# A two-block transformer layer on one core: projections as one 512-column matmul per high weight tile instead of two of 256, with VectorE adding the two PSUM halves

## The chip, the core and the metric

The kernel runs on one core of one Trainium2 chip. The metric is the time of one execution in device microseconds (us). The core's engines work side by side: TensorE (PE in the profile; PEld is its loading of weights), VectorE (DVE), ScalarE (ACT), GpSimd (POOL), and SyncE (SP), which only issues transfers. Weights come from HBM by DMA into SBUF; TensorE writes its sums to PSUM, 8 banks of 512 float32 columns on 128 partitions.

## The reference

A sequence of 256 positions with 2048 features goes through two transformer blocks. Each normalizes x, projects it to many heads, runs several attention or recurrence branches, mixes them with gates, and adds the result to x. The first block also has a feed-forward part with a convolution over three positions. Cut to what matters here:

```python
h = rmsnorm(x, norm_attn[l])
... = jnp.split(h @ w_in[l], split_at, axis=-1)     # 2048 x (some 120 column blocks of 128)
o_nsa, o_sb, o_hg = nsa_mixer(...), stick_breaking(...), hgrn2(...)
merged = jnp.sum(gsig * jnp.einsum('btnc,ncd->btnd', branches, w_branch[l]), axis=2)
x = x + merged @ w_out[l]
u = rmsnorm(x, norm_ffn[l]) @ w_up[l]                # 2048 x 11264
c = conv_b + sum(shifted(u, j) * conv_w[j] for j in range(3))
x = x + (silu(gate) * val) @ w_down[l]               # gate, val = split(c)
# second block: rms_norm, h @ w_in_2, four attention kinds, gates, w_branch_2, w_out_2, final norm
```

All is float32 and must come out nearly so.

## The kernel before

**Products in three parts.** TensorE takes its operands as float32r (a reduced float32). To keep the precision, each weight tile w and each activation tile h is split into a high and a low part, w = whi + wlo and h = HH + HL. A product is whi·HH + whi·HL + wlo·HH. `mm3` (L511 to L515) issues these three matmuls for one weight tile of 128 x 128: L513 (whi with the high activations), L514 (whi with the low ones), L515 (wlo with the high ones), each with 256 columns, since an activation tile is 128 features x 256 positions. Each loads its 128 x 128 weights first (LDWEIGHTS in the profile), so whi is loaded twice.

**Blocks.** All weights are laid out in 470 blocks of 128 x 2048 floats (1 MB), streamed through a ring of 4 slots. Block n holds 16 weight tiles. In a projection of 2048 features (KT = 16 tiles) one block gives 128 output columns: 16 calls of `mm3`, 48 matmuls, summed in one half of a PSUM bank, `gps[0]` or `gps[1]` in turn (named gemm in the profile). That is the inner loop of `project` (L522 on). `pair` and `early` do the same for the first blocks after a normalization, on the activations before their factor (UH, UL in place of HH, HL); `early` puts some of its blocks in the banks M (mix). Other products (w_branch with 8 feature tiles, w_down, w_branch_2 with 4) also use `mm3`.

**What goes with a block.** SyncE issues the load of block n+4 when TensorE is done with block n (`reload`, semaphore gemm_done). ScalarE makes whi of block n+3 from the loaded block (L943, `split`), then takes the finished sum of block n out of PSUM (`take`: L966, L981, L992 with a sigmoid, or L1262 for w_up), which counts the semaphore evac_done. VectorE makes wlo of block n+3 (L1413). TensorE starts block n once wlo of it is there (lo_ready) and the sum of block n-2, which was in the same bank, is out (evac_done). The order on each engine is fixed by the program: `advance(k)` on each engine's side does k blocks' worth of this upkeep between pieces of attention work, and each engine takes its instructions strictly in order.

**Where the projection's result goes elsewhere.** For w_out the sum is added to x by VectorE (`residual`, L1711). For w_up (88 blocks) ScalarE takes the centre tap of the convolution out of PSUM (L1262) and VectorE the two others (L1765, L1766). The first 8 blocks of w_in, w_up and w_in_2 go through VectorE's `early`: a multiplication by the norm's factor on the way out of PSUM (L1465).

**Other places named below.** The linear recurrence (hgrn2) runs in 8 levels with HG_STEP = 3 blocks beside each; L1669, L1670 end it, and `operand` (L1678) makes the low parts of the branches' outputs. The norm's sums of squares are L1477, L1478, its factor L1441, the low part of the normalized activations L1448.

## Time and profile before

| | |
|---|---|
| median of 3 runs | 2945.47 us (2942.90 to 2945.55) |
| span of the profiled execution, first to last instruction | 2942.8 us |
| TensorE matmuls | busy 2867.0 us, 97% of the span, 23642 recorded |
| weight loads | busy 2842.7 us |
| VectorE | busy 1622.2 us, 55% |
| ScalarE | busy 1306.6 us, 44% |
| DMA | 545.92 MB, mean 186 GB/s |

The profiled execution's own time is its span and 2 to 3 us around it: the runs' median lies 2.7 us above the span. A matmul's duration in the profile is a latency: the next one starts long before it ends. How fast TensorE works is read from start to start. "Idle before" names what an engine waited for.

### The profile page before, as it was taken

The numbers are of one execution on the slowest core, as the hardware profiler recorded it, in microseconds if no ns is written. First come the engines' busy times: TensorE is split into PE (matmuls) and PEld (weight loads), VectorE is DVE, ScalarE is ACT, GpSimd is POOL, SyncE is SP. The second block draws the span as 40 slices with busy tenths as digits, with TensorE's granted clock in tenths as the row PEclk, the third lists the DMA queues.
The fourth block names the chain that finished last, engine by engine and source line by source line (L and its number), as shares of the span: only waits on it lengthen the run. The fifth ranks groups of instructions, "written<-read, shape, count | busy, mean of one in ns | idle before, by whom it ended". The sixth has DMA issues, their size and how long they took to land.

```text
span 2942.8 us, 55782 instructions
## 1 busy us (share of the span) xinstructions
PE 2867.0 (97%) x23642; PEld 2842.7 (97%) x23642; DVE 1622.2 (55%) x1573; ACT 1306.6 (44%) x1387; POOL 159.7 (5%) x125
## 2 busy tenths in 40 slices
PE   7897999999999999999999999999999999999997
PEld 6897899999999999999999999999999999999997
DVE  6443544466544677766666545554444554546575
ACT  3353446664443444444444333343334444445442
POOL 4000000000000001000000000010000000000330
PEclk9999899999999999999999999999999999999999
DMA  6556444445545655455554555455554455555853
GB/s 204 182 185 181 148 149 144 158 170 175 170 174 214 236 193 200 176 182 185 185 178 180 216 185 195 177 190 184 185 180 164 163 204 203 184 193 207 285 209 129
DMA packets 94836, 545.92 MB, mean 186 GB/s; under 512 B 11528, under 2 KB 25992, under 8 KB 34288
## 3 DMA queue, kind: packets, MB, share of 16 engines
q1 hardware_dynamic: 84768, 511.01, 49.0%
q0 software_dynamic: 9936, 32.92, 3.9%
q8 instruction: 111, 1.82, 0.2%
q14 instruction: 21, 0.17, 0.0%
HBM read 519.44 MB, written 24.38 MB: 185 GB/s over the span
## 4 chain that ended last, share of the span: by engine, by line
PE 93%; DVE 3%; DMA 3%; ACT 0%; issue 0%; DVEq 0%; SPq 0%; ACTq 0%
PE gemm L513 26%; PE gemm L515 26%; PE gemm L514 26%; PE mix L513 4%; PE mix L515 4%; PE mix L514 4%; DMA raw<-wstream 2%; DVE wlo L1413 1%; PE mix L760 1%; PE mix L600 1%; DMA XT<-xT 0%; PE mix L696 0%; PE mix L885 0%; ACT whi L943 0%; DVE cbuf L1765 0%
## 5 line engine op out<-in xcount | busy, mean ns | idle before, releaser
L1413 DVE TENSOR_TENSOR wlo<-raw,whi 128x2048 fp32r<-128x2048 f32 x470 | 1095.7, 2332 | 1069.2 <-ACT whi L943 1068.4
L513 PE MATMUL gemm<-HH,whi 128*128 128x256 f32 x5728 | 1634.1, 285 | 15.6 <-issue 10.8
L514 PE MATMUL gemm<-HL,whi 128*128 128x256 f32 x5728 | 1623.4, 283 | 0.0
L515 PE MATMUL gemm<-HH,wlo 128*128 128x256 f32 x5728 | 1623.4, 283 | 0.0
L943 ACT ACTIVATE whi<-raw 128x2048 fp32r<-128x2048 f32 x470 | 898.6, 1912 | 1388.5 <-DMA raw<-wstream 1385.3
L513 PEld LDWEIGHTS gemm<-HH,whi 128*128 128x128 f32 x5728 | 1101.9, 192 | 22.1 <-issue 14.8
L514 PEld LDWEIGHTS gemm<-HL,whi 128*128 128x128 f32 x5728 | 1102.3, 192 | 0.7 <-issue 0.7
L515 PEld LDWEIGHTS gemm<-HH,wlo 128*128 128x128 f32 x5728 | 1101.8, 192 | 0.0
L513 PE MATMUL mix<-ACTH,whi 128*128 (+1 forms) x528 | 149.4, 283 | 0.0
L514 PE MATMUL mix<-ACTL,whi 128*128 (+1 forms) x528 | 149.4, 283 | 0.0
L515 PE MATMUL mix<-ACTH,wlo 128*128 (+1 forms) x528 | 149.4, 283 | 0.0
L513 PE MATMUL gemm<-OH,whi 128*128 128x256 f32 x384 | 108.7, 283 | 0.0
L514 PE MATMUL gemm<-OL,whi 128*128 128x256 f32 x384 | 108.7, 283 | 0.0
L515 PE MATMUL gemm<-OH,wlo 128*128 128x256 f32 x384 | 108.7, 283 | 0.0
L513 PEld LDWEIGHTS mix<-ACTH,whi 128*128 128x128 f32 x528 | 101.4, 192 | 0.0
L514 PEld LDWEIGHTS mix<-ACTL,whi 128*128 128x128 f32 x528 | 101.4, 192 | 0.0
L515 PEld LDWEIGHTS mix<-ACTH,wlo 128*128 128x128 f32 x528 | 101.4, 192 | 0.0
L513 PE MATMUL gemm<-UH,whi 128*128 128x256 f32 x192 | 57.6, 300 | 22.3 <-DVE wlo L1413 16.9
L513 PEld LDWEIGHTS gemm<-OH,whi 128*128 128x128 f32 x384 | 73.7, 192 | 0.0
L514 PEld LDWEIGHTS gemm<-OL,whi 128*128 128x128 f32 x384 | 73.7, 192 | 0.0
L515 PEld LDWEIGHTS gemm<-OH,wlo 128*128 128x128 f32 x384 | 73.7, 192 | 0.0
L513 PE MATMUL mix<-YH,whi 128*128 128x256 f32 x256 | 72.4, 283 | 0.0
(363 smaller groups left out, 2666.1 us busy)
## 6 DMA issues: line engine op xcount, KB each, us to landing
raw<-wstream SPq DMA_DIRECT2D x470, 1024.0 KB, 4.9
scratch<-gate_scratch POOLq DMA_DIRECT2D x12, 512.0 KB, 5.2
gate_scratch<-scratch SPq DMA_DIRECT2D x32, 128.0 KB, 3.9
GL<-gate_scratch POOLq DMA_DIRECT2D x8, 512.0 KB, 5.1
gate_scratch<-arena SPq DMA_DIRECT2D x32, 128.0 KB, 3.8
bias_scratch<-arena POOLq DMA_DIRECT2D x1, 3328.0 KB, 45.9
btile<-bias_scratch POOLq DMA_DIRECT2D x21, 128.0 KB, 2.4
XT<-xT SPq DMA_DIRECT2D x4, 512.0 KB, 9.0
```

The source lines that it names most:

```text
L513: pe.matmul(ps, whi[slot][:, w], mh, start=first, stop=False, **kw)
L514: pe.matmul(ps, whi[slot][:, w], ml, start=False, stop=False, **kw)
L515: return pe.matmul(ps, wlo[slot][:, w], mh, start=False, stop=last, **kw)
L600: return pe.transpose(ps, src, ident[p0:p0 + n, p0:p0 + n])
L760: ins = pe.matmul(M[:, i // 4, (i % 4) * P:(i % 4) * P + P], x, x, start=True, stop=True)
L943: f(whi[slot][:, :], raw[slot][:, :], ACT.Copy).then_inc(s["hi_ready"], 1)
L1413: tt(wlo[slot][:, :], raw[slot][:, :], whi[slot][:, :].bitcast(F32), ALU.subtract).then_inc(s["lo_ready"], 1)
```

## The change

For every projection of 16 feature tiles, the two matmuls on whi become one: the high and the low activation tile are streamed one behind the other, 512 columns, against one load of whi. Their products land in the two halves of a PSUM bank. wlo with the high activations (256 columns) is added to the first half, as before. `mm2` does this; to allow a single access pattern over both tiles, HH and HL (and each UH, UL) become parts of one tensor, HX (UX). The products of w_branch, w_down and w_branch_2 keep `mm3`.

The two halves then have to be added. VectorE does it in `join`, a tensor_reduce over pairs that lie 256 columns apart, as it takes the sum out of PSUM. So all the evictions that ScalarE did for these projections move to VectorE, and stand in its order ahead of wlo of block n+3. In the sigmoid case ScalarE still applies the sigmoid, in SBUF. For w_up VectorE joins into `btile`, and ScalarE and VectorE read the taps from there. `early` joins first and multiplies then, and `residual` adds in two steps. GpSimd's load of one bias row into `btile` waits until w_up is done. HG_STEP goes from 3 to 4.

```diff
-HG_STEP = 3
+HG_STEP = 4
-        HH = at("HH", [P, KT, T], o_hh, F32R)
-        HL = at("HL", [P, KT, T], o_hl, F32R)
+        HX = at("HX", [P, 2 * KT, T], o_hh, F32R)
+        HH, HL = HX[:, 0:KT, :], HX[:, KT:2 * KT, :]
...
+        def halves(bank):
+
+            return bank.rearrange("p (c t) -> p t c", c=2)
...
+            pool.wait_ge(s["f_taps"], N_UP)
             bias(R_FOX, i)
...
+            def mm2(bank, w, mh, mx, slot, first, last):
+
+                def high():
+                    return pe.matmul(bank.rearrange("p (c t) -> p c t", c=2), whi[slot][:, w], mx, start=first, stop=last)
+
+                def low():
+                    return pe.matmul(bank[:, 0:T], wlo[slot][:, w], mh, start=False, stop=False)
+
+                if last:
+                    low()
+                    return high()
+                high()
+                return low()
...
+                            if kt == KT:
+                                ins = mm2(gps[bank][:, :], cols(k), mh(k), ml(k), slot, k == 0, k == KT - 1)
+                            else:
+                                ins = mm3(gps[bank][:, c * T:(c + 1) * T], cols(c * kt + k),
+                                          mh(k), ml(k), slot, k == 0, k == kt - 1)
...
+            def xk(k):
+                return HX[:, k::KT, :]
...
             def to_scratch(began):
+
                 def take(n, bank, i, j, it):
-                    act.wait_ge(s["gemm_done"], n + 1)
-                    f(tile(i + dst0), gps[bank][:, 0:T], ACT.Copy).then_inc(s["evac_done"], 1)
+
+                    c = i + began
+                    act.wait_ge(s["evac_done"], c + (use(B_G0) + 1))
+                    d = SCR[:, c * T:(c + 1) * T] if isinstance(i, int) else SCR[:, bass.ds(c * T, T)]
+                    f(d, d, ACT.Sigmoid).then_inc(s["g0_sig"], 1)
                 return take
...
+            stages = ((0, B_G0, lambda i: None), (B_G0, B_Y, to_scratch), (B_B, B_Y2, lambda i: None))
...
+            def join(dst, bank):
+
+                return dve.tensor_reduce(dst, halves(bank), AX, ALU.add)
+
+            def to_arena(dst0):
+                def take(n, u0, i, j):
+                    dve.wait_ge(s["gemm_done"], n + 1)
+                    join(tile(i + dst0), gps[(u0 + j) % 2][:, :]).then_inc(s["evac_done"], 1)
+                return take
...
-                    tt(A[:, j, :] if take is None else btile[j % 2][:, 0:T], early_bank(r, j), rstd[:, :], ALU.mult
-                       ).then_inc(s["evac_done"], 1)
+                    d = A[:, j, :] if take is None else btile[j % 2][:, 0:T]
+                    me.link(join(d, early_bank(r, j)))
+                    tt(d, d, rstd[:, :], ALU.mult).then_inc(s["evac_done"], 1)
...
-                    tt(d, d, gps[(u0 + j) % 2][:, 0:T], ALU.add).then_inc(s["evac_done"], 1)
+                    bank = gps[(u0 + j) % 2]
+                    me.link(tt(d, d, bank[:, T:2 * T], ALU.add))
+                    tt(d, d, bank[:, 0:T], ALU.add).then_inc(s["evac_done"], 1)
...
+                    dve.wait_ge(s["gemm_done"], it * 4 + (B_UP + j + 1))
+                    join(btile[j % 2][:, 0:T], gps[(u0 + j) % 2][:, :]).then_inc(s["evac_done"], 1)
                     ahead(it * 4 + (B_UP + j), (B_UP + j) % RING, it + (B_UP + j) // RING)
+                    dve.wait_ge(s["evac_done"], it * 4 + (u + j + 1))
```

On TensorE, the first weight tiles of the program (UH and UL are the high and low activations, whi and wlo the weight parts) stand so before:

```order
L513 MATMUL gemm<-UH_80,whi_53 128x256
L514 MATMUL gemm<-UL_83,whi_53 128x256
L515 MATMUL gemm<-UH_80,wlo_57 128x256
L513 MATMUL gemm<-UH_80,whi_53 128x256
L514 MATMUL gemm<-UL_83,whi_53 128x256
L515 MATMUL gemm<-UH_80,wlo_57 128x256
```

and now, at the end of the first block and the start of the next (UX holds both activation parts):

```order
L527 MATMUL gemm<-UX_79,whi_53 128x512
L530 MATMUL gemm<-UX_79,wlo_57 128x256 x2
L527 MATMUL gemm<-UX_79,whi_53 128x512
L527 MATMUL gemm<-UX_79,whi_54 128x512
L530 MATMUL gemm<-UX_79,wlo_58 128x256
```

Three instructions per weight tile become two with the same 768 columns in sum; in a block's last tile the low part goes first.

On VectorE, after the first norm factor of the feed-forward part (its `early`, where btile receives a block's product and cbuf the convolution) before:

```order
L1441 RECIPROCAL rstd<-rstd 128x256
L1465 TENSOR_TENSOR btile_89<-gemm,rstd 128x256
L1765 SCALAR_TENSOR_TENSOR cbuf<-btile_89,vec,cbuf 128x255
L1766 SCALAR_TENSOR_TENSOR cbuf<-btile_89,vec,cbuf 128x254
L1465 TENSOR_TENSOR btile_90<-gemm,rstd 128x256
L1413 TENSOR_TENSOR wlo_58<-raw_50,whi_54 128x2048
```

and now:

```order
L1486 RECIPROCAL rstd<-rstd 128x256
L1432 TENSOR_REDUCE btile_85<-gemm 128x256
L1512 TENSOR_TENSOR btile_85<-btile_85,rstd 128x256
L1811 SCALAR_TENSOR_TENSOR cbuf<-btile_85,vec,cbuf 128x255
L1812 SCALAR_TENSOR_TENSOR cbuf<-btile_85,vec,cbuf 128x254
L1432 TENSOR_REDUCE btile_86<-gemm 128x256
L1512 TENSOR_TENSOR btile_86<-btile_86,rstd 128x256
L1407 TENSOR_TENSOR wlo_58<-raw_50,whi_54 128x2048
```

One tensor_reduce (the join) stands ahead of each multiplication, and wlo behind it.

In the loop over the other 80 blocks of w_up, VectorE's block before (register instructions between):

```order
L1413 TENSOR_TENSOR wlo_57<-raw_49,whi_53 128x2048
L1764 REGISTER_ALU
L1765 ISA
L1765 SCALAR_TENSOR_TENSOR cbuf<-gemm,vec,cbuf 128x255
L261 ISA
L1766 ISA
L1766 SCALAR_TENSOR_TENSOR cbuf<-gemm,vec,cbuf 128x254
```

and now:

```order
L1432 TENSOR_REDUCE btile_85<-gemm 128x256
L1406 REGISTER_ALU
L1407 TENSOR_TENSOR wlo_57<-raw_49,whi_53 128x2048
L1839 REGISTER_ALU
L1810 REGISTER_ALU
L1811 ISA
L1811 SCALAR_TENSOR_TENSOR cbuf<-btile_85,vec,cbuf 128x255
L267 ISA
L1812 ISA
L1812 SCALAR_TENSOR_TENSOR cbuf<-btile_85,vec,cbuf 128x254
```

The join comes first in the block, and the taps read btile in SBUF, no more the PSUM bank.

## Rows read from the trace of the kernel before

**Rows 1.** The page: busy time by engine, and the chain that ended last.
```profile
PE 2867.0 (97%) x23642; PEld 2842.7 (97%) x23642; DVE 1622.2 (55%) x1573; ACT 1306.6 (44%) x1387; POOL 159.7 (5%) x125
...
PE 93%; DVE 3%; DMA 3%; ACT 0%; issue 0%; DVEq 0%; SPq 0%; ACTq 0%
```
**Rows 2.** Page, costliest groups: out<-in, shapes, xcount | busy us, mean ns | idle before.
```profile
L1413 DVE TENSOR_TENSOR wlo<-raw,whi 128x2048 fp32r<-128x2048 f32 x470 | 1095.7, 2332 | 1069.2 <-ACT whi L943 1068.4
L513 PE MATMUL gemm<-HH,whi 128*128 128x256 f32 x5728 | 1634.1, 285 | 15.6 <-issue 10.8
L943 ACT ACTIVATE whi<-raw 128x2048 fp32r<-128x2048 f32 x470 | 898.6, 1912 | 1388.5 <-DMA raw<-wstream 1385.3
```
**Rows 3.** Matmul groups, shapes apart (weights 128*rows, output 128xcolumns); same columns.
```profile
L513 PE MATMUL gemm<-UH,whi 128*128 128x256 f32 x192 | 57.6, 300 | 22.3 <-DVE wlo L1413 16.9 <-DVE UL L1453 4.0 <-DVE XR L1815 1.4
L513 PE MATMUL mix<-UH,whi 128*128 128x256 f32 x192 | 54.6, 285 | 0.4 <-DVE wlo L1413 0.4
L515 PE MATMUL gemm<-HH,wlo 128*128 128x256 f32 x5728 | 1623.4, 283 | 0.0
```
**Rows 4.** Timeline of TensorE in a projection: start us, duration us.
```profile
700.00 0.28 PE L513 MATMUL gemm<-HH,whi 128*128 128x256 f32 x1
700.12 0.28 PE L514 MATMUL gemm<-HL,whi 128*128 128x256 f32 x1
700.24 0.28 PE L515 MATMUL gemm<-HH,wlo 128*128 128x256 f32 x1
```
**Rows 5.** Timeline of TensorE, float32r with 128 columns on 30 weight columns.
```profile
213.29 0.22 PE L629 MATMUL mix<-whi,blkH 128*30 128x128 f32 x1
213.35 0.22 PE L630 MATMUL mix<-whi,blkL 128*30 128x128 f32 x1
213.41 0.22 PE L631 MATMUL mix<-wlo,blkH 128*30 128x128 f32 x1
```
**Rows 6.** Timeline of TensorE, plain float32 with 512 columns.
```profile
173.41 5.31 PE L616 MATMUL mix<-scratch,cst 128*128 128x512 f32 x12
```
**Rows 7.** Matmul groups, the last float32r matmul before a wait (no load behind it).
```profile
L515 PE MATMUL gemm<-UH,wlo 128*128 128x256 f32 x1 | 0.3, 279 | 0.0
```
**Rows 8.** Busy us (xcount) of PE, PEld, DVE, ACT, POOL in windows; clock, DMA.
```profile
1300.00:1400.00 100.00, 100.00 (x836) 100.00 (x835) 64.60 (x79) 47.42 (x54) 0.00 (x0) 1.00 0.51 180
```
**Rows 9.** VectorE groups, shapes apart.
```profile
L1495 DVE TENSOR_REDUCE st<-scratch 128x2 f32<-128x512 f32 x12 | 8.2, 686 | 0.4
L1693 DVE TENSOR_TENSOR arena<-gemm,scratch 128x512 f32 x8 | 5.5, 692 | 18.5 <-PE gemm L515 18.5
L1711 DVE TENSOR_TENSOR arena<-arena,gemm 128x256 f32 x24 | 10.1, 420 | 32.9 <-PE gemm L515 32.9
```
**Rows 10.** VectorE's timeline in the loop over w_up, [idle before <-releaser].
```profile
1220.59 2.29 DVE L1413 TENSOR_TENSOR wlo<-raw,whi 128x2048 fp32r<-128x2048 f32 x1 [1.95 <-ACT whi L943]
```
**Rows 11.** VectorE's timeline, first blocks of w_up.
```profile
1156.13 4.17 DVE L1413 TENSOR_TENSOR wlo<-raw,whi 128x2048 fp32r<-128x2048 f32 x1
...
1164.40 2.28 DVE L1413 TENSOR_TENSOR wlo<-raw,whi 128x2048 fp32r<-128x2048 f32 x1
...
1187.04 1.22 DVE L1448 TENSOR_TENSOR HL<-arena,HH 128x1024 fp32r<-128x1024 f32 x1
```
**Rows 12.** TensorE's timeline, starts of blocks 5, 6 and 9 of w_up.
```profile
1160.35 0.39 PE L513 MATMUL mix<-UH,whi 128*128 128x256 f32 x1
...
1166.74 0.39 PE L513 MATMUL mix<-UH,whi 128*128 128x256 f32 x1 [0.38 <-DVE wlo L1413]
...
1184.12 0.35 PE L513 MATMUL gemm<-HH,whi 128*128 128x256 f32 x1
```
**Rows 13.** VectorE's timeline at the end of the recurrence.
```profile
817.34 2.35 DVE L1669 SCALAR_TENSOR_TENSOR arena<-arena,vec 128x2048 f32<-128x2048 f32 x1 [3.37 <-ACT arena L1197]
...
828.80 2.29 DVE L1678 TENSOR_TENSOR OL<-arena,OH 128x2048 fp32r<-128x2048 f32 x1 [1.98 <-ACT OH L1207]
```
**Rows 14.** VectorE's timeline, last block of the program.
```profile
2926.99 0.42 DVE L1711 TENSOR_TENSOR arena<-arena,gemm 128x256 f32<-128x256 f32 x1 [4.15 <-PE gemm L515]
```

More of the change, by code:

```diff
@@ L929, in _ @@
                 ins.then_inc(s["gemm_done"], 1)
-            pair(B_O2, s["mg_l"], [(N_Y + i + 1, 4 * i + 4) for i in range(N_Y2)], hk, lk)
-            project(B_O2 + 2, N_O - 2, hk, lk)
+            pair(B_O2, s["mg_l"], [(N_Y + i + 1, 4 * i + 4) for i in range(N_Y2)], hk, xk)
+            project(B_O2 + 2, N_O - 2, hk, xk)
             norm_sums(3)
@@ L1177, in _ @@
             decays(0)
-            advance(3)
+            advance(HG_STEP)
             for lv in range(1, 8):
@@ L1249, in conv @@
             def conv(n, bank, i, j):
-                first = isinstance(i, int) and i < EARLY
-                if first:
-                    act.wait_ge(s["evac_done"], use(B_UP) + i + 1)
-                else:
-                    act.wait_ge(s["gemm_done"], n + 1)
-                product = btile[j % 2][:, 0:T] if first else gps[bank][:, 0:T]
+                act.wait_ge(s["evac_done"], i + (use(B_UP) + 1))
+                product = btile[j % 2][:, 0:T]
                 v0 = V_CONV + 4 * i
@@ L1419, in ahead @@
                 split(n + AHEAD, s2 % RING, turn + s2 // RING)
+            loop = [0]
             def plain(n0, count, u0=0, take=None, per=0):
@@ L1423, in body @@
                     if take:
+                        loop[0] = turn - (n0 + j) // RING
                         take(n, u0, i, j)
@@ L1431, in _, with to_gates @@
             at = [0]
[L1433 to L1436 removed]
+            def join(dst, bank):
[5 more added lines that the diff above has]
+                return take
+            def to_gates(n, u0, i, j):
+                dve.wait_ge(s["gemm_done"], n + 1)
+                join(gates[:, :], gps[(u0 + j) % 2][:, :]).then_inc(s["evac_done"], 1)
@@ new lines, in to_ring, with take @@
+            def to_ring(layer, began):
+                def take(n, u0, i, j):
+                    dve.wait_ge(s["gemm_done"], n + 1)
+                    r = (j + began) % 4
+                    turns = (j + began) // 4 + layer * 2 * N_G // 4
+                    if not isinstance(i, int):
+                        dve.wait_ge(gate_out[r], (loop[0] + turns) * 16)
+                    elif turns:
+                        dve.wait_ge(gate_out[r], turns * 16)
+                    join(gring[layer][r], gps[(u0 + j) % 2][:, :]).then_inc(s["evac_done"], 1)
+                return take
@@ new lines, in to_scratch, with take @@
+            def to_scratch(began):
+                def take(n, u0, i, j):
+                    dve.wait_ge(s["gemm_done"], n + 1)
+                    c = i + began
+                    if isinstance(i, int) and c >= 12:
+                        dve.wait_ge(gate_out[c % 4], 2 * N_G // 4 * 16)
+                    d = SCR[:, c * T:(c + 1) * T] if isinstance(i, int) else SCR[:, bass.ds(c * T, T)]
+                    join(d, gps[(u0 + j) % 2][:, :]).then_inc(s["evac_done"], 1)
+                return take
@@ new lines, in _ @@
+            stages = ((0, N_NSA - 1, to_arena), (N_NSA - 1, B_SB, lambda i: to_gates),
+                      (B_SB, B_CW, lambda i: to_arena(20 + i)), (B_CW, B_SB2, lambda i: None),
+                      (B_SB2, B_G, lambda i: to_arena(20 + N_SB1 + i)), (B_G, B_G0, lambda i: to_ring(0, i)),
+                      (B_G0, B_Y, to_scratch),
+                      (B_B, B_Z, to_arena), (B_Z, B_G2, lambda i: to_arena(58 + i)), (B_G2, B_Y2, lambda i: to_ring(1, i)))
+            def advance(count):
+                while count:
+                    first, end, take = [x for x in stages if x[0] <= at[0] < x[1]][0]
+                    n = min(count, end - at[0])
+                    plain(at[0], n, use(at[0]), take(at[0] - first))
+                    at[0] += n
+                    count -= n
@@ L1757, in taps @@
             def taps(u, i, j, pair):
-                first = isinstance(i, int) and i < EARLY
-                product = btile[j % 2][:, 0:T] if first else gps[(u0 + j) % 2][:, 0:T]
-                done = "f_taps" if first else "evac_done"
+                product = btile[j % 2][:, 0:T]
                 v0 = V_CONV + 4 * i
@@ L1772, in taps @@
                     me.link(tt(e[:, :], e[:, :], cbuf[:, b, 0, :], ALU.mult))
-                    dve.wait_ge(s[done], i + 1 if first else u + 1)
+                    dve.wait_ge(s["f_taps"], i + 1)
                     tt(cbuf[:, b, 0, :], e[:, :], cbuf[:, b, 1, :], ALU.mult).then_inc(s["f_act"], 1)
@@ L1996, in _ @@
             dve.wait_ge(s["x2_back"], 64)
-            plain(B_O2, N_O, use(B_O2), residual(3, XT2), 2)
+            plain(B_O2, N_O, use(B_O2), residual(3, XT2), 3)
             factor(3)
```

77 lines of the change are left out of this document (24 added, 53 removed).

## The prediction, made before the changed kernel was run

> **What bounds the kernel now.** I read the page's busy shares and the chain of waits first. TensorE is busy 97% of the span and holds 93% of the chain, VectorE 3% and DMA 3% [rows 1]. So what TensorE has to stream sets the time, and the other engines matter only where their work comes late. In the costliest groups the reader sees who is waited for: wlo (VectorE, 470 times 2.33 us) waits for whi nearly all of its idle time, and whi (ScalarE) waits for the loaded blocks [rows 2]. ScalarE and VectorE both have room.
>
> The second question is how long one matmul holds TensorE. Its duration of 0.28 us is a latency; in the timeline the next one starts 0.12 us later, whether it repeats the same whi with the low activations or takes wlo [rows 4]. The window of 100 us holds 836 of them [rows 8], 119.6 ns each, at granted clock 1.00 (the 2.4 GHz level). A weight tile's three matmuls are thus 360 ns and a block of 16 tiles 5.76 us. Per column that is 120/256 = 0.469 ns.
>
> **The change on TensorE.** The merged form stands where the projections have 16 feature tiles: 5728 + 192 + 192 = 6112 weight tiles [rows 2, 3], 382 blocks. Each gives up one weight load and one matmul instruction, and streams the same 768 columns. What a tile saves is therefore 240 ns less what one matmul of 512 columns takes from start to start. No row of before shows a float32r matmul of 512 columns, so I bound it.
>
> - Upper bound of the pitch, 240 ns (gain 0). The time goes with columns alone, if 0.469 ns is the rate at which float32r operands stream. The rows nearest to this: float32r matmuls of 128 columns, on only 30 weight columns, start 60 ns apart [rows 5], which is 0.469 ns per column again. Half the columns take exactly half the time; a fixed part per instruction, say 13 ns, would have made them 66. And a load of 30 columns instead of 128, for half the stream, has changed nothing in the rate, which it should if loads took read bandwidth from the stream.
> - Lower bound, about 213 ns, one column per 2.4 GHz cycle. For it: plain float32 matmuls of 512 columns, 12 instructions in 5.31 us [rows 6], at most 442 ns each, and if each passes the array twice, 0.43 ns per column and pass. So the array itself can go faster than 0.469. [...]
> - Between: the load slows the stream that it lies beside. The one float32r matmul with no load behind it lasts 279 ns against 283 [rows 3, 7]. If the 4 ns are the load's, the second half of the 512 columns, with no load beside it, saves some 4 to 14 ns: pitch 226 to 236.
>
> I take 240, since the row with half the columns is the same mode and excludes a fixed part. Term: 0. Each ns by which I am wrong is worth 6112 x 1 ns = 6.1 us; 4 to 14 ns are 24 to 86 us, 24 ns (216 instead of 240) are 147 us.
>
> The Trainium skill ("TensorE: Matmul & The Clock Gate", Back-to-back issue gap) states N/2.4 + 2.5 ns as the isolated spacing of a matmul with N columns. For 256 that is 109 ns, where the trace has 120 [rows 4]: it does not hold for this mode. By it the 512 columns would take 216. The same page (in its part on loading weights) says that weights have a read port of their own and take nothing from the running stream; the trace agrees as far as rows 5 reach, and it speaks against the case between.
>
> **The change on VectorE.** A join reads 512 columns from PSUM and writes 256. The trace has no such instruction. Nearest: a reduction of 512 columns from SBUF, 686 ns, and an addition over 512 columns out of PSUM, 692 ns [rows 9]. I take 0.69 us. The strided pairs could make it dearer, by at most about a factor of two (1.3 us, each half read on its own and the overhead paid twice); cheaper than the 0.42 us of a 256-column operation [rows 9] it can't be. The number, counted in the code: 213 evictions that ScalarE did for the projections, 80 of w_up and 24 in `early` make 317, x 0.69 = 219 us; the 32 residual blocks get a second addition, 32 x 0.42 = 13 us. VectorE goes from 1622 to about 1855 us, 63%. In the w_up loop, the fullest long stretch, it waits 1.95 us per block for whi [rows 10]; a join of 0.69, even of 1.3, fits in. It is hidden in steady stages: a block's bank is needed only one block (5.76 us) after the sum is done, and wlo(n+3) only three blocks after block n. ScalarE gets lighter, so whi comes no later.
>
> HG_STEP = 4 moves a block's upkeep earlier in each level of the recurrence, GpSimd's wait for f_taps moves a bias load behind w_up. Neither is on the path; the cover is TensorE's own stream of 23 us per 4 blocks. Term: 0.
>
> Not hidden, as wlo comes late already in these places:
> - The first blocks of w_up. After the late norm factor VectorE works off a backlog; one wlo takes 4.17 us there, and ends at 1160.30, where block 5 starts at 1160.35; block 6 starts at 1166.74, right behind the next wlo [rows 11, 12]. Two joins stand ahead of the first: 2 x 0.69 = +1.4; one more ahead of the second, +0.7. Both shift the program by about 2.1 us. Block 9 starts at 1184.12 and needs, for its last four tiles, the low activations that end at 1188.26; tile 12 is due at 1184.12 + 12 x 0.36 = 1188.44 [rows 11, 12], slack 0.2. Joins 2 to 8, seven, now stand ahead: 7 x 0.69 = 4.8, less the 2.1 shift and the slack: +2.5. Together some +5 us.
> - The end of the recurrence, where 2.35 and 2.29 us pieces and their ScalarE counterparts alternate [rows 13] and a join stands between: at most two joins, +1.3.
> - The last block of the program: the second addition lies bare, +0.4 [rows 14].
> - Other waits behind single joins (start of the attention parts, first block): +1, a guess from one or two joins of 0.69.
>
> Sum: 0 + 5 + 1.3 + 0.4 + 1 = about +8 us on the span of 2942.8, so 2951. The runs' median lies 2.7 above the profiled span, but the profiled execution itself is the fast end of them (2942.90), so in terms of the median I write 2952. With joins of 1.3 us the same sum gives about +13.
>
> **Rivals.**
> 1. The merged matmul streams at one column per cycle, 216 ns: -147, and +8 for the stalls: about 2806. For: the plain float32 rate [rows 6]. Against: rows 5, where half the columns take half of 120. By the skill's formula above this would be the result.
> 2. The load beside the stream costs something: pitch 226 to 236, -24 to -86 and +8: 2870 to 2930, centre 233 (-43), about 2910. For: 279 against 283 [rows 3, 7]; against: rows 5. These two end on the other side, faster. The point from which they decide is a pitch of 238.7 ns: below it the saving exceeds the 8 us.
> 3. Pitch 240, but the new stalls are absorbed (the backlog at w_up is caught by the block's own slack): 2943 to 2950, no change.
> 4. The join is much dearer than its neighbours in the trace. It becomes the bound of the w_up loop only above about 1.95 us, the idle time per block [rows 10]; for 80 blocks each 0.1 us beyond is 8 us. At 1.5 us it is not the bound but lengthens every backlog: w_up's first blocks +10, others +5: 2965 or more. Nothing in rows 9 speaks for it beyond the stride.
> 5. That the change doesn't do what it says: the order of instructions shows one instruction for two on every such tile, so only its price is open.
>
> **How the numbers follow.** Columns alone (pitch 240): 0.52, of which the stalls show as slower 0.33 (my forecast, 2952, own range 2946 to 2965), are absorbed 0.17, and 0.02 for a small gain from the freed ScalarE. Load beside stream: 0.27 (0.24 faster, 0.03 same). Full rate: 0.17. Dear join: 0.04. About 0.2% (6 us) is what a measurement of this kernel can tell from no change. Faster 0.02 + 0.24 + 0.17 = 0.43; same 0.17 + 0.03 = 0.20; slower 0.33 + 0.04 = 0.37. The range leaves out the full rate and the ends of the others: 2875 to 2972.
>
> **What would show it.** In a steady window of w_up the start-to-start of the 512-column matmul: 240 (forecast), 226 to 236, or 216. The pace of blocks there: 5.76, 5.54 to 5.7, or 5.38 us. The join's mean: 0.69. TensorE's idle time behind wlo at the start of w_up: some 5 us more. VectorE's wait for whi per block in w_up: about 1.3 instead of 1.95. A pitch below 238 ns, or joins over 1.3 us, makes the forecast wrong.

## The result: 2926.4 us, 17.8 us faster, from a gain of 41 us and a loss of 23

| | before | after |
|---|---|---|
| median | 2944.18 us | 2926.39 us (2920.17 to 2927.45) |
| ratio, 95% interval | | 0.9936 (0.9922 to 0.9950) |
| span of the profiled execution | 2942.8 us | 2925.6 us |

The page after: busy time by engine, and the groups that answer to [rows 1 to 3].

```profile
PE 2827.9 (97%) x17530; PEld 2518.4 (86%) x17530; DVE 1870.2 (64%) x1955; ACT 1250.5 (43%) x1159; POOL 154.5 (5%) x125
...
L527 PE MATMUL gemm<-HX,whi 128*128 128x512 f32 x5728 | 2027.6, 401 | 30.2 <-issue 12.3
L530 PE MATMUL gemm<-HX,wlo 128*128 128x256 f32 x5728 | 1555.1, 282 | 0.0
...
L1407 DVE TENSOR_TENSOR wlo<-raw,whi 128x2048 fp32r<-128x2048 f32 x470 | 1086.0, 2311 | 384.5 <-ACT whi L970 383.7
```

TensorE is as full as before, with 6112 matmuls and loads fewer. VectorE has 248 us more; the forecast was 233. Whether the stream got faster is again read from start to start. TensorE's timeline after, in the loop over w_up:

```profile
1300.00 0.40 PE L527 MATMUL gemm<-HX,whi 128*128 128x512 f32 x1
1300.24 0.28 PE L530 MATMUL gemm<-HX,wlo 128*128 128x256 f32 x1
1300.35 0.40 PE L527 MATMUL gemm<-HX,whi 128*128 128x512 f32 x1
...
1301.06 0.40 PE L527 MATMUL gemm<-HX,whi 128*128 128x512 f32 x1
```

Three tiles take 1.06 us, 353 ns each and not 360: over such a stretch the 512 columns hold TensorE 236 ns on average and the 256 of wlo 117. In the stretches with attention work between the blocks it is less, about 347 (231 + 116):

```profile
502.15 0.39 PE L527 MATMUL gemm<-HX,whi 128*128 128x512 f32 x1
502.38 0.28 PE L530 MATMUL gemm<-HX,wlo 128*128 128x256 f32 x1
502.50 0.39 PE L527 MATMUL gemm<-HX,whi 128*128 128x512 f32 x1
...
503.54 0.39 PE L527 MATMUL gemm<-HX,whi 128*128 128x512 f32 x1
```

The window that answers to [rows 8] holds 569 matmuls, two per tile, where 836 were three per tile; VectorE is at 77 us of 100, up from 65:

```profile
1300.00:1400.00 100.00, 100.00 (x569) 86.80 (x568) 77.22 (x99) 47.81 (x52) 0.00 (x0) 1.00 0.51 183
```

At 7 to 12 ns per tile, 6112 tiles give 43 to 73 us. Only 17.8 came out, so something took the rest. TensorE's waits after, by what ended them (us in total, times, longest):

```profile
PE gemm L527 <- DVE wlo L1407: 21.4, 3, 14.3
PE mix L723 <- ACT scratch L1119: 21.2, 1, 21.2
...
PE gemm L527 <- DVE arena L1432: 6.9, 2, 4.1
PE gemm L527 <- DVE scratch L1432: 6.0, 2, 3.4
...
PE mix L527 <- DVE wlo L1407: 3.2, 1, 3.2
PE mix L605 <- DVE gates L1538: 2.3, 1, 2.3
PE mix L627 <- DVE scratch L1987: 2.2, 1, 2.2
PE mix L656 <- DVE wlo L1407: 1.9, 1, 1.9
```

Before, the first two of these stood there with 19.5 and the same 21.2 us. The whole list adds up to 84.4 us, before to 62.4. The two rows on L1432, the join, are new: 12.9 us in four waits. The longest shows the mechanism. VectorE's timeline there, and TensorE's:

```profile
181.96 3.67 DVE L1572 SCALAR_TENSOR_TENSOR arena<-arena,vec,scratch 128x2048 f32<-128x2048 f32 x3 [8.60 <-ACT scratch L1070]
185.67 3.87 DVE L1584 TENSOR_TENSOR blkF<-arena,vec 128x240 f32<-128x240 f32 x8
189.44 0.69 DVE L1432 TENSOR_REDUCE arena<-gemm 128x256 f32<-128x512 f32 x1
```
```profile
190.28 0.77 PE L527 MATMUL gemm<-HX,whi 128*128 128x512 f32 x1 [4.10 <-DVE arena L1432]
...
191.06 0.63 PE L527 MATMUL gemm<-HX,whi 128*128 128x512 f32 x1
...
191.70 0.63 PE L527 MATMUL gemm<-HX,whi 128*128 128x512 f32 x1
```

VectorE takes its instructions in order. The join stands behind 7.5 us of attention work, the bank stays full, and TensorE waits 4.1 us for it. In the kernel before, the same pieces ran on VectorE (3.68 and over 3 us), but ScalarE emptied the bank in between, and TensorE did not wait:

```profile
185.58 1.90 ACT L943 ACTIVATE whi<-raw 128x2048 fp32r<-128x2048 f32 x1
187.38 0.37 ACT L966 ACTIVATE arena<-gemm 128x256 f32<-128x256 f32 x1
```

The wait has a second price, TensorE's clock. Behind the 4.1 us without work a pair takes 0.64 us from start to start (191.06 to 191.70), and not 0.35, until 193.6. The windows show the granted clock (the third figure from the end) there, and back at 1.00 behind it; the last line is the kernel before at the same time, without a wait:

```profile
190.00:192.00 2.00, 1.72 (x5) 1.56 (x6) 2.00 (x2) 1.41 (x2) 0.00 (x0) 0.55 0.29 123
...
194.00:196.00 2.00, 2.00 (x14) 1.75 (x13) 2.00 (x2) 0.00 (x0) 0.00 (x0) 1.00 0.04 8
```
```profile
190.00:192.00 2.00, 2.00 (x20) 2.00 (x18) 2.00 (x6) 2.00 (x3) 0.00 (x0) 1.00 0.19 33
```

So the granted clock fell from the 2.4 GHz level to the 1.2 GHz level. Five pairs took 3.34 us there in place of 1.77: this wait cost 4.1 us and then 1.6 us more. All four waits for a join in this execution have such a stretch beside them.

The time can be dated by blocks: SyncE issues the load of block n+4 the moment TensorE is done with block n. Difference to the kernel before, in us, at the end of some blocks (merge alone and joins alone are experiments below):

| end of block | time before | changed kernel | merge alone | joins alone | what lies between |
|---|---|---|---|---|---|
| 16 | 139.2 | -3.1 | -3.5 | -1.9 | |
| 26 | 201.9 | +1.5 | -4.3 | +3.6 | the wait shown above |
| 76 | 563.4 | -4.6 | -8.5 | +3.3 | attention |
| 84 | 617.0 | -0.7 | -9.8 | +6.6 | start of the recurrence |
| 124 | 883.2 | -2.7 | -15.6 | +10.2 | recurrence and its end |
| 166 | 1125.7 | -4.3 | -16.6 | +10.6 | w_branch, w_out |
| 178 | 1196.1 | -0.6 | -17.4 | +16.1 | first blocks of w_up |
| 256 | 1645.8 | -9.5 | -25.4 | +15.6 | rest of w_up |
| 300 | 1899.3 | -9.5 | -25.4 | +15.6 | w_down, unchanged |
| 396 | 2483.4 | -20.2 | -36.2 | +15.6 | second block's projections |
| 429 | 2692.4 | -16.9 | -41.7 | +20.4 | attention, its gates |
| 465 | 2904.1 | -17.2 | -42.2 | +23.1 | |

### The profile page after: what moved, and what is told of

It is laid out like the page before. It is cut to its first block, busy times and chain, and to the rows that moved or that the text cites. A ratio compares the mean times of both kernels' runs of the same rounds, so it can differ in the third digit from the quotient of the medians.

```text
span 2925.6 us, 43772 instructions
## 1 busy us (share of the span) xinstructions
PE 2827.9 (97%) x17530; PEld 2518.4 (86%) x17530; DVE 1870.2 (64%) x1955; ACT 1250.5 (43%) x1159; POOL 154.5 (5%) x125
## 4 chain that ended last, share of the span: by engine, by line
PE 91%; DVE 3%; DMA 3%; ACT 2%; issue 0%; POOL 0%; DVEq 0%; SPq 0%; ACTq 0%
PE gemm L527 46%; PE gemm L530 23%; PE mix L520 3%; PE mix L522 3%; PE mix L521 3%; DMA raw<-wstream 3%; PE gemm L521 2%; PE gemm L522 2%; PE gemm L520 2%; PE mix L527 1%; PE mix L787 1%; DVE wlo L1407 1%; PE mix L627 1%; PE mix L530 1%; ACT whi L970 0%
## 5 line engine op out<-in xcount | busy, mean ns | idle before, releaser
L527 PE MATMUL gemm<-HX,whi 128*128 128x512 f32 x5728 | 2027.6, 401 | 30.2 <-issue 12.3
L530 PE MATMUL gemm<-HX,wlo 128*128 128x256 f32 x5728 | 1555.1, 282 | 0.0
L527 PEld LDWEIGHTS gemm<-HX,whi 128*128 128x128 f32 x5728 | 1066.6, 189 | 266.8 <-issue 25.3
L530 PEld LDWEIGHTS gemm<-HX,wlo 128*128 128x128 f32 x5728 | 1089.2, 190 | 29.8 <-issue 0.7
L1432 DVE TENSOR_REDUCE arena<-gemm 128x256 f32<-128x512 f32 (+1 forms) x173 | 119.6, 691 | 314.7 <-PE gemm L527 314.6
L527 PE MATMUL gemm<-UX,whi 128*128 128x512 f32 x192 | 74.5, 427 | 22.6 <-DVE wlo L1407 17.0
L1432 DVE TENSOR_REDUCE btile<-gemm 128x256 f32<-128x512 f32 x84 | 57.9, 690 | 40.9 <-PE gemm L527 40.6
L1432 DVE TENSOR_REDUCE scratch<-gemm 128x256 f32<-128x512 f32 x48 | 33.2, 691 | 73.1 <-PE gemm L527 61.0
```

Of the source, the lines that this page charges most:

```text
L527: return pe.matmul(bank.rearrange("p (c t) -> p c t", c=2), whi[slot][:, w], mx, start=first, stop=last)
L530: return pe.matmul(bank[:, 0:T], wlo[slot][:, w], mh, start=False, stop=False)
L1432: return dve.tensor_reduce(dst, halves(bank), AX, ALU.add)
```

## The experiments

Times of one group are compared with runs of the kernel before made beside them (2943.8 to 2945.9 us).

**Merge alone.** The kernel before, with the merged matmuls; all evictions as they were, so the product in the second half of the bank is left out of the result.

```diff
-ins = mm3(gps[bank][:, c * T:(c + 1) * T], cols(c * kt + k),
-          mh(k), ml(k), slot, k == 0, k == kt - 1)
+ins = mm2(gps[bank][:, :], cols(k), mh(k), ml(k), slot, k == 0, k == KT - 1)
 ...
 f(tile(i + dst0), gps[bank][:, 0:T], ACT.Copy)      # as before
```

> The kernel before with the merged matmuls of the change and nothing else of it: ScalarE takes the first half of the bank as before, HG_STEP stays 3. The product whi x HL, in the second half, is left out of the result. Theory (the merge gives 6.8 to 8 ns on each of 6112 tiles, and the joins in VectorE's queue give back over half of it): 2944 - 42 to 52, so 2892 to 2902 us. Rival (the merge itself is worth only what the changed kernel shows, the joins cost nothing): 2926. Stalls of TensorE over 1 us stay the same as in the kernel before.

Measured: 2902.72 against 2943.77 us, ratio 0.9851 (0.9826 to 0.9876): 41.0 us faster, just short of the theory's 42 to 52. Its page counts the same matmuls, and VectorE as before:

```profile
PE 2819.0 (97%) x17530; PEld 2509.6 (87%) x17530; DVE 1620.7 (56%) x1573; ACT 1305.9 (45%) x1387; POOL 158.3 (5%) x125
```

TensorE's waits for the join are gone from its list, as there is none. The others did not all stay the same, as I had expected: one for wlo grew from 0.7 to 2.3 us, and the list adds up to 67.6 us against 62.4.

**Joins alone.** The changed kernel with the high and low tile as two matmuls again.

```diff
 def high():
-    return pe.matmul(bank.rearrange("p (c t) -> p c t", c=2), whi[slot][:, w], mx, start=first, stop=last)
+    pe.matmul(bank[:, 0:T], whi[slot][:, w], mx[:, 0, :], start=first, stop=False)
+    return pe.matmul(bank[:, T:2 * T], whi[slot][:, w], mx[:, 1, :], start=False, stop=last)
```

> The changed kernel with everything but the merge: the high and the low activation tile go as two matmuls of 256 columns, each with its load of whi, into the two halves of the bank, and VectorE joins them. Theory (joins behind long pieces of attention work hold the bank): slower than before by 20 to 35 us, 2964 to 2979. Rival (joins are hidden, as forecast but for 8 us): 2952 or less. The stalls behind L1432 stand at the same places as in the changed kernel, each shorter by at most 0.2 us.

Measured: 2966.57 us, ratio 1.0072 (1.0055 to 1.0089): 22.8 us slower, within the theory's 20 to 35. With the 41.0 of the merge that is -18.2, the change's -17.8. The two parts add up. (This kernel has HG_STEP = 4 too; that part is tried below.) Its waits for the join, at the same places as in the changed kernel:

```profile
PE gemm L527 <- DVE arena L1433: 6.1, 2, 3.8
PE gemm L527 <- DVE scratch L1433: 5.2, 2, 3.0
```

The four are 0.3 to 0.5 us shorter than after (11.3 us against 12.9), where I expected at most 0.2. That TensorE, with longer blocks, comes to them later and finds more of VectorE's work done would explain it; it was not tried by itself.

**What the two parts consist of.** The profiled executions of the four kernels can be taken apart with the list of TensorE's waits and the granted clock. The share lost at the lower level, 0.45, is an estimate from the pair's 0.64 us against 0.35.

| us | before | merge alone | joins alone | changed kernel |
|---|---|---|---|---|
| span | 2942.8 | 2900.2 | 2966.4 | 2925.6 |
| TensorE's waits, the whole list | 62.4 | 67.6 | 80.2 | 84.4 |
| TensorE at work at the 1.2 GHz level | 23.8 | 24.8 | 35.4 | 45.7 |
| of this lost, 0.45 of it | 11 | 11 | 16 | 21 |
| the rest, mostly its stream at 2.4 GHz | 2870 | 2821 | 2870 | 2821 |

The merged matmuls shorten the stream by 48 to 50 us, 8 ns per tile, whether the joins are there or not; of this the merge alone gives back some 5 us in longer waits. The joins leave the stream as it is. They cost 18 us of waits and about 5 us of lower clock, which is nearly all of the 23.6 us between the two spans.

**HG_STEP = 3.**

```diff
-HG_STEP = 4
+HG_STEP = 3
```

> The changed kernel with HG_STEP = 3. Theory (the step only moves where the waits in the recurrence fall): 2926, within 3 us. Rival (4 was needed, since the joins make each level longer): 2932 or more. If 3 is better, the stall of 2.7 us at 870 us is the step's doing: 2922.

Measured: 2917.68 us (2916.57 to 2919.03), 8.7 us less than the changed kernel. No theory had this size. By the blocks' ends only 0.9 us is gained at block 126, behind the recurrence: the wait of 2.6 us at its end is gone, as the expectation had it, and another of 1.2 us for a join stands at 828 us. Up to block 407 3.7 us more come, where the wait of 2.2 us for L1987 shown above does not occur, and 3.8 more up to block 456. The later places run the same program in both. The waits account for 2.9 us of the profiled difference of 8.4; the rest is mostly the clock: TensorE is at work at the 1.2 GHz level for 37.2 us in place of 45.7 (about 4 us by the same estimate), with no such stretch at blocks 124, 406 and 454. Executions of one kernel differ in this too: the four of the merge alone took 2893.17 us at a mean granted clock of 0.993, 2902.11 at 0.990, and 2903.34 and 2906.43 at 0.988. HG_STEP = 4 was not needed; how much of the 8.7 us is the step's own is open.

**The stream by itself.** TensorE alone, 96 matmuls of one shape in a row.

```diff
+for i in range(96):
+    pe.matmul(G[:, bank(), :], w(whi), h(2), start=True, stop=True)      # 512 columns; the others alike
```

> A kernel of its own, which leaves out the layer: TensorE streams float32r matmuls in runs of 96 of one shape each (160 more of the first shape ahead), start to start is read from its trace. The runs: 256 columns on 128 weight columns; 512 contiguous; 512 out of two tiles that lie apart; 512 with whi and 256 with wlo in turn; 384; 128; then 256 columns on 64 and on 32 weight columns; 512 and 128 columns on 32; then 512 and 256 in turn with VectorE computing wlo beside it, and again with 1 MB loads arriving. At the end VectorE alone: joins of a bank's halves, joins of neighbouring columns, additions of 256 columns with one operand in PSUM, and with both in SBUF. Theory 1 (each weight load takes about 7 ns from the stream beside it, in proportion to its weight columns, and a column costs 0.441 ns; both fitted to 120 ns before and 353 ns for a pair after): 120, 233, 233, pair 353, 176, 64, then 117, 115, 228, 58. Theory 2 (7 ns per matmul whatever it loads): the same with 128 weight columns, but 120, 120, 233, 64 with fewer. Theory 3 (columns alone, 0.469 ns, as in the prediction): 120, 240, 240, 360, 180, 60, 120, 120, 240, 60. If VectorE or the loads take from TensorE's reads, the last two pairs are longer than the quiet one; I expect no difference over 2 ns. Joins 0.69 us in either layout, additions 0.42.

Its groups (busy us and mean ns stand behind the bar; the pitch is the busy time less one latency, over 95; in L226's row the 256-column matmuls of L227 stand between):

```profile
L226 PE MATMUL gemm<-HX,whi 128*128 128x512 f32 x96 | 34.0, 399 | 0.0
L237 PE MATMUL gemm<-HX,whi 128*32 128x512 f32 x96 | 22.4, 394 | 0.0
L221 PE MATMUL gemm<-HX,whi 128*128 128x512 f32 x96 | 21.9, 389 | 0.0
L229 PE MATMUL gemm<-HX,whi 128*128 128x384 f32 x96 | 16.8, 334 | 0.0
L219 PE MATMUL gemm<-HX,whi 128*128 128x256 f32 x96 | 11.7, 283 | 0.0
L233 PE MATMUL gemm<-HX,whi 128*64 128x256 f32 x96 | 11.1, 276 | 0.0
L235 PE MATMUL gemm<-HX,whi 128*32 128x256 f32 x96 | 11.0, 276 | 0.0
L231 PE MATMUL gemm<-HX,whi 128*128 128x128 f32 x96 | 10.8, 275 | 0.0
L239 PE MATMUL gemm<-HX,whi 128*32 128x128 f32 x96 | 5.9, 223 | 0.0
```

| columns | on 128 weight columns | on 64 | on 32 |
|---|---|---|---|
| 512 | 227 (two far tiles too) | | 232 |
| 384 | 173.7 | | |
| 256 | 120.0 | 113.5 | 113.3 |
| 128 | 111.1 | | 60.0 |
| 512 and 256 in turn | 236.0 + 117.2 | | |

(ns from start to start, means over 95 in the trace.) All three theories fall. A column costs 0.443 ns (227/512, 113.4/256) where the weights cost nothing, not 0.469. Over 128 weight columns 128 columns take 111 ns, where 60 are enough over 32: there the loads set the pace. 256 columns over 128 weight columns take 6.5 ns more than over 64, 384 take 3.4 ns more than 0.443 per column, and 512 nothing more. So before the change TensorE was held a little by its weight loads, and 512 columns over one load are free of that. How a load does it is not shown: a spacing of 111 ns alone would leave a stream of 113 as it is. Its price is neither proportional (64 weight columns already cost nothing) nor fixed. With VectorE at work beside the stream the pair took 237.2 + 116.6, with loads of 263 GB/s 236.7 + 116.6: no difference over 2 ns, as I expected. The join took 692 ns, the same over neighbouring columns; an addition with one operand in PSUM 420.

**Orders of the stream.**

```diff
+hi(0, b, True)
+for g in range(0, 16, group):
+    for k in range(g, g + group):
+        lo(k, b)
+    for k in range(g + 1, min(g + group + 1, 15)):
+        hi(k, b)
+return hi(15, b, last=True)
```

> A kernel of its own again, which leaves out the layer. The first study measured 227 ns for 512 columns in a row and 120 for 256, but 236 + 117 = 353 for the two in turn (in a pattern that repeats every three pairs), where 227 + 113 or 120 would make 340 or 347. This one asks what the alternation costs and whether an order avoids it. Runs of 96, all float32r: 512 columns accumulating in one bank; 512 with whi and 512 with wlo in turn; 512 and 256 in turn without accumulation, in different banks. Then blocks of 16 tiles, accumulating, six each, with the low products in groups of 1, 2, 4, 8 and 16 between the high ones. Then 256 columns on 112 and on 96 weight columns; 512 on 128 in turn with 256 on 64; and the three matmuls of the kernel before. Theory A (a weight load of 128 columns needs 111 ns itself, as 128 columns on 128 show; a 256-column stream of 113 ns just covers it and pays up to 7 ns; the change of length costs a few ns at each turn): 227 accumulating; 454 for the two of 512; turns cost 353 whatever bank; groups of 16 give (16 x 227 + 16 x 120) / 16 = 347 per tile and groups between lie between 347 and 353; 112 weight columns about 115, 96 about 113; the pair with 64 weight columns 340; three matmuls 360. Theory B (accumulation in PSUM is what makes 236 of 227): 236 accumulating, 340 to 347 for the pair without accumulation, no difference between the groups.

Accumulating in one bank 227.0; whi and wlo in turn with 512 columns each 226.7; in turn 512 and 256 without accumulation 236.6 + 116.6. That refutes theory B: neither the bank nor accumulation makes 236 of 227. A block of 16 tiles, from start to start: 5.654 us in turn, 5.574 in groups of 2, 5.614 of 4, 5.587 of 8, 5.567 of 16, which is 353.4 ns and 347.9 ns per tile at the two ends, as theory A had it. Groups of 2 (348.4) come nearly down to those of 16, groups of 4 (350.9) do not; nothing in the theory says why. The three matmuls of the kernel before took 360, as it had.

Two of its parts need a second look. 512 columns on 128 weight columns in turn with 256 on 64 took 340.0, exactly 227 + 113. So the change of length costs nothing by itself; it costs where 256 columns stand over 128 weight columns. And 256 columns on 112 weight columns took 117.8, on 96 116.0, where it had 115 and 113: the price falls step by step with the weight columns, and a load that just fits under its stream is not the whole of it. Windows over the turns (first) and the groups of 16 (second) show the two orders in counts:

```profile
118.00:151.00 33.00, 33.00 (x189) 28.64 (x188) 0.00 (x0) 0.00 (x0) 0.00 (x0) 1.00 0.00 1
...
253.00:285.00 32.00, 32.00 (x187) 28.36 (x187) 0.00 (x0) 0.00 (x0) 0.00 (x0) 1.00 0.00 1
```

**Four joins moved ahead.** One of the four places:

```diff
             ins.then_inc(s["nsa_qk"], 1)
+            pull()          # the join of the next block, without its wlo
             dve.wait_ge(s["nsa_qk"], 1)
```

> The changed kernel, HG_STEP 4, with four single joins moved ahead of a long piece of attention work on VectorE, nothing else: after the gains of the first attention's operands (before the 8 additions into blkF), before the wait for the recurrence's logarithm, between the two operands' low parts, and between the reciprocal and the multiplication behind the differential attention. Theory (a join that stands behind such a piece holds the bank, and TensorE waits): the four stalls of 4.1, 3.4, 2.6 and 2.8 us go or shrink to under 1 us each, 2926 - 10 to 13 = 2913 to 2917. Rival (the same time is lost a little later, to wlo or to the attention's own work): 2922 or more.

Measured: 2915.23 us, ratio 0.9899 (0.9883 to 0.9916), 11.2 less than the changed kernel's 2926.39. The time is the theory's; that all four waits would shrink to under 1 us did not come true. At the place shown above TensorE now waits 0.20 and then 0.93 us:

```profile
185.71 0.47 PE L527 MATMUL gemm<-HX,whi 128*128 128x512 f32 x1 [0.20 <-DVE arena L1433]
192.42 0.48 PE L527 MATMUL gemm<-HX,whi 128*128 128x512 f32 x1 [0.93 <-DVE arena L1433]
```

The wait between the operands (2.6 us) is gone. But two of the four only moved: the next join is the one waited for, 2.4 us in the recurrence and 4.6 us at the second block's gates.

```profile
PE gemm L527 <- DVE gates L1433: 4.6, 1, 4.6
...
PE gemm L527 <- DVE scratch L1433: 2.4, 1, 2.4
```

The list of waits is 5.0 us shorter than the changed kernel's. About as much again is the clock: TensorE is at work at the 1.2 GHz level for 33.0 us in place of 45.7, and behind the first place the granted clock stays at 1.00.

**Three matmuls in the first 8 blocks of w_up.**

```diff
-me.link(join(d, early_bank(r, j)))
-tt(d, d, rstd[:, :], ALU.mult).then_inc(s["evac_done"], 1)
+tt(d, early_bank(r, j)[:, 0:T], rstd[:, :], ALU.mult).then_inc(s["evac_done"], 1)      # r == 1
```

> The changed kernel with the first 8 blocks of w_up as before the change: three matmuls per tile, and no join ahead of the multiplication by the norm's factor. Theory (the joins lengthen VectorE's backlog there, and TensorE's waits of 3.4 and 1.1 us are theirs): minus 3.5 to 4.5 us for the waits, plus 8 x 0.11 = 0.9 for the stream: 2922 to 2924. Rival (the backlog is GpSimd's traffic, as a wlo of 4.2 us showed before): no change, 2926 or 2927.

Measured: 2917.86 us (2910.44 to 2920.76), 8.5 us less. That is more than the 2.4 to 4.4 expected. TensorE's wait for wlo there fell from 3.2 to 0.2 us and the other (0.9) went, and by the blocks' ends 3.6 us are gained up to block 178, as expected. The rest arises later, where the program is the same. There the stretches at the 1.2 GHz level behind the waits at blocks 301, 406 and 428 do not occur in this execution; in all TensorE is at work at that level for 33.2 us in place of 45.7.

```profile
PE mix L520 <- DVE wlo L1413: 0.2, 1, 0.2
```

**All three.**

```diff
-HG_STEP = 4
+HG_STEP = 3             # with the four pulls and the three matmuls
```

> The four joins moved ahead, three matmuls in the first 8 blocks of w_up, and HG_STEP = 3. Theory (the three effects add up): 2917.7 - 10 to 13 - 3 = 2902 to 2905, about what the merge without any join took (2902.7). Rival (they overlap, since each hides another's lateness): 2910 or more.

Measured: 2909.15 us, ratio 0.9880 (0.9863 to 0.9896). 4 us short of the theory and just at the rival's edge: the single gains of 11.2, 8.5 and 8.7 do not add. The waits add up to 72.5 us, 11.9 fewer than after, and TensorE is at work at the 1.2 GHz level for 31.6 us, 14.1 fewer. The three single changes each shed 8.5 to 12.7 us of that level, and the stretch at block 406 is among them in all three, so part of each gain is the same one.

**Grouped order in the changed kernel.**

```diff
+pe.matmul(two, whi[slot][:, cols(0)], mx(0), start=True, stop=False)
+for k in range(KT):
+    pe.matmul(bank[:, 0:T], wlo[slot][:, cols(k)], mh(k), start=False, stop=False)
+for k in range(1, KT):
+    ins = pe.matmul(two, whi[slot][:, cols(k)], mx(k), start=False, stop=k == KT - 1)
```

> The changed kernel, HG_STEP 4, with another order inside a block and nothing else: one matmul of 512 columns, then the 16 of 256 on wlo, then the other 15 of 512. It holds for all projections but the first block after each normalization and those whose inputs come in pieces. Theory (the alternation of lengths costs TensorE 5.4 ns per tile, 353.4 against 347.9 in the kernel of its own): about 365 blocks x 16 x 5.4 = 32 us less stream; the waits behind the joins grow by up to a block's difference, some us: 2926 - 26 to 32 = 2894 to 2900. Rival (VectorE's and ScalarE's lateness takes it up, as it took most of the merge's gain): 2905 or more.

Measured: 2903.47 us, ratio 0.9854 (0.9837 to 0.9871), 22.9 less than the changed kernel, under the 26 to 32 expected; the rival (2905 or more) missed it too. The window of [rows 8] now holds 577 matmuls against 569. From block 178 to 256 the order gains 6.7 us, 5.4 ns per tile, as the theory had it. From block 16 to 166, where the attention lies between blocks, it gains only 4.7 us in nearly twice as many blocks. Of this, 1.7 us were lost again at block 32, to a longer wait with a stretch of lower clock beside it; for the rest, the pairs there already ran at 347 ns in part (timeline at 502 us above), and an order that gives 347.9 has nothing to win. My term had counted 353 everywhere.

```profile
1300.00:1400.00 100.00, 100.00 (x577) 88.37 (x575) 78.59 (x99) 48.92 (x55) 0.00 (x0) 1.00 0.52 189
```

**Everything together**, with a second join moved ahead in three of the places.

```diff
+            pull()          # a second one behind the logarithm's use, behind blkF, and at the gates
```

> HG_STEP 3, three matmuls in the first 8 blocks of w_up, the grouped order, and seven joins moved ahead (the four of before, a second one in three of the places, where the trace showed the next join as the one waited for). Theory (effects add up): 2909 - 30 for the order - 4 to 6 for the second joins = 2873 to 2876. Rival (as the stream gets shorter, VectorE and the loads bound more places): 2885 or more.

Measured: 2887.89 us (2883.26 to 2888.99), ratio 0.9802 (0.9789 to 0.9815): 56.7 us faster than the kernel before, 38.5 than the changed one, and the best of the study. It missed my 2873 to 2876 and lies where the rival had it (2885 or more): the order gave about 21 instead of 30, and the second pulls gave little. TensorE still waits for joins (4.5 us in three waits, 12.9 after) and again for wlo, which the pulled joins now stand ahead of:

```profile
PE gemm L541 <- DVE wlo L1428: 5.1, 3, 2.7
...
PE gemm L541 <- DVE scratch L1454: 2.9, 1, 2.9
...
PE gemm L541 <- DVE arena L1454: 1.6, 2, 1.4
```

## Why the prediction was wrong

**The step that failed** is the first term: "I take 240, since the row with half the columns is the same mode and excludes a fixed part." In place of 240 the trace has 236, and the following 256 columns fell from 120 to 117, which no term had. The term was not 0 but -41 us (merge alone), and the stream by itself became 48 us shorter. The argument compared 120 ns for 256 columns on 128 weight columns with 60 ns for 128 on 30, and took the exact half for proportionality. It was a coincidence of two different extras: without any, 256 columns take 113.4 ns and 128 would take 56.7. One row had 6.6 ns that go with its 128 weight columns, the other some 3 of its own. I changed two sizes at once between the rows, and read one cause. The same proportionality made the forecast of slower; my own chances had faster at 0.43 against 0.37 for slower, and the single figure did not follow them.

**The case between** came nearest: I gave it 0.27, with a pitch of 226 to 236 and a gain of 24 to 86 us before the waits. That its 41 us lie so near its centre of 43 is in part luck. The 512 columns stood at the end of its range (236), and 3 ns of the 7 came from the 256 columns behind them, which it left at 120. Its evidence, 279 against 283 ns [rows 3, 7], pointed the right way. That the load has a price is shown (120.0 ns on 128 weight columns, 113.5 on 64); that it is paid to the stream beside it is not, since 512 columns pay nothing. **The full rate** (216) was refuted: 227 is the least that 512 columns took, alone and without any alternation. It leaned on a plain float32 matmul that passes the array twice, which no run here shows.

By the isolated spacing that the Trainium skill ("TensorE: Matmul & The Clock Gate", Back-to-back issue gap) gives, the 512 columns would take 216 ns. The stream by itself measured 227. The same page (Step-by-step: what each phase is for) says of SBUF's read ports that a load takes nothing from the running stream. The runs agree for 512 columns, whose 227 ns on 128 weight columns are twice the 113.5 of 256 on 64. For 256 columns the time does go with the weight columns (120.0 on 128, 113.5 on 64); the runs do not show whether a read port has a part in that.

**The join's price** was right (0.69 us; measured 0.691), its number was not: the trace has 350 joins, not 317. ScalarE's evictions for the projections outside w_up were 246, not 213. The price was hidden in steady stages: in w_up VectorE still idles 0.43 to 0.60 us before each wlo, and 1.0 us before the join of every second block.

**The waits behind it** were mis-sized: +8 us in the sum, 22.8 measured, of which about 5 are the lower clock behind the waits, a term that the prediction did not have. Point by point (losses by the blocks' ends, so with the clock's part):

- First blocks of w_up: +5 forecast. Joins alone lose 5.5 us there (from +10.6 to +16.1). The size is right, but not by the stated terms alone: the waits of 2.5 and 1.9 us are followed by a stretch of lower clock, and behind the norm's factor VectorE's first two multiplications by it, now from SBUF to SBUF, took 2.0 and 1.9 us in place of 0.42 each, while the next wlo took 2.3 in place of 4.17.
- End of the recurrence: +1.3 forecast. Joins alone lose 3.6 from block 84 to 124, a wait of 2.2 us and a stretch of lower clock. Too small.
- Last block: +0.4; the last wait grew from 1.9 to 2.3 us. Right.
- "Other waits behind single joins", +1. This hid the real loss: 5.5 us up to block 26 (from -1.9 to +3.6), 3.3 at the start of the recurrence (block 84), 4.8 between blocks 396 and 429 and 2.7 after. The sentence "a block's bank is needed only one block (5.76 us) after the sum is done" holds where VectorE's queue is short. I looked for places where wlo came late before, and not for those where more than 5.7 us lie ahead of a join, in work or in VectorE's own waiting: at the start of the recurrence it waits 12.1 us for ScalarE (L1167) and works 3.5, and the join at 607.89 stands behind both. For wlo, made three blocks ahead, such a stretch was harmless; for the bank it is not.

The sum of the working, 0 + 8, is thus -41 + 23. The forecast of slower was wrong in sign; the range, which reached into the case between, held the time, though with a gain and a loss that both were not in the sum.

Of the signs that I named, the pitch (236) and the pace in w_up (16 x 353 = 5.65 us per block) told the case at once, and the join's mean (0.691) cleared it of blame. VectorE's wait for whi in w_up was 0.4 to 0.6 us and not 1.3: part of its idle time now lies before the join.

## What to carry to other kernels

When an operation's eviction moves to another engine, list what stands ahead of it in that engine's order, not the engine's busy share: here 0.69 us of work cost TensorE up to 4.1 us of wait, at 64% busy. Count the clock with it: behind that wait TensorE lost 1.6 us more at the 1.2 GHz level. Two rows that differ in two sizes can't bound a rate; the pitch of a shape that no trace shows is best measured by itself, in one run of 0.3 ms. And when matmuls of two lengths alternate, try them in groups: it was worth 23 us here, more than the change itself.

## What the runs showed of the hardware

- Float32r columns stream at 0.443 ns each at granted clock 1.00 (227 ns for 512); 128 columns on 128 weight columns take 111 ns, on 32 60; 256 columns take 120.0 on 128 weight columns, 117.8 on 112, 116.0 on 96 and 113.5 on 64.
- 512 and 256 columns in turn take 353 ns, where 227 and 120 in groups take 347. The pattern repeats every three pairs (240, 120, 236, 114, 232, 118). With the 256 columns on 64 weight columns the pair took 340.0 in every turn. In the layer the pair took 347 in some stretches and 353 in others. What chooses between the two is open.
- Behind waits of TensorE of some 2 to 5 us the granted clock was at the 1.2 GHz level for a while: the 512 and 256 columns took 0.64 us there, 0.35 at the 2.4 GHz level. Not every such wait has it. The wait of 2.3 to 2.4 us at the start of w_in_2 (block 301) stands in all of the layer's kernels; the granted clock fell behind it in the changed kernel (0.55 from 1900 to 1903 us) and not in the one before (1.00 from 1909 to 1912 us).
- 512 columns on 32 weight columns took 232 ns, more than on 128 (227). Not explained.
- The multiplication by the norm's factor now reads SBUF and writes SBUF. In the changed kernel 8 of its 24 executions took 1.9 to 2.0 us, the other 16 0.43 us. GpSimd was at work during all of the 8 and none of the 16. Before, when it read PSUM, all 24 took 0.41 to 0.43 us, 9 of them with GpSimd at work. That the two engines hold each other up in SBUF fits; it was not tried by itself. The row shows 16 of the 24, the lines below one of the 8:

```profile
L1512 DVE TENSOR_TENSOR arena<-arena,rstd 128x256 f32<-128x256 f32 x16 | 16.0, 1000 | 0.6
```
```profile
1146.60 2.01 DVE L1512 TENSOR_TENSOR btile<-btile,rstd 128x256 f32<-128x256 f32 x1
```
```profile
1145.93 10.04 POOL L384 TENSOR_TENSOR arena<-arena,rstd 128x1024 f32<-128x1024 f32 x4 [11.72 <-DVE rstd L1486]
```
